# Attention output of a FoX layer: from three matmul passes over V to two, with an add behind

## The chip, the core and the metric

The kernel runs on one NeuronCore of a Trainium2 chip. Its time is the device time of one execution, in microseconds (us), and lower is better. The core's engines run side by side and meet only at semaphores: TensorE (PE in the rows; PEld is its weight load), VectorE (DVE), ScalarE (ACT), GpSimd (POOL) and the DMA queue of SyncE (SP).

## What is computed

Two layers on x of 1 x 512 x 1024 floats. Layer 0 mixes tokens by a Conformer convolution, layer 1 by the forgetting attention below; a squared-ReLU MLP of width 4096 follows each. There are 16 heads of 64 columns.

```python
def forgetting_attention(h, w_in, b_f, w_o):
    proj = h @ w_in
    q, k, v = proj[..., :D], proj[..., D:2*D], proj[..., 2*D:3*D]
    F = cumsum(log_sigmoid(proj[..., 3*D:] + b_f), axis=1)
    ...
    s = einsum("bhqd,bhkd->bhqk", q_blk, k) * HEAD_DIM ** -0.5
    s = s + (f_blk[..., None] - F[:, :, None, :])
    s = where(kpos <= qpos, s, -1e30)
    p = softmax(s, axis=-1)
    return einsum("bhqk,bhkd->bhqd", p, v)
    ...
    return o @ w_o
```

## The kernel before

Matmul operands are single precision, split in two: the high part (`...hi`) is a copy rounded to TensorE's reduced float format, and the rest (`...lo`) is the value minus that copy. ScalarE makes the high part, VectorE the rest, and a product is three passes on TensorE: high x high, high x rest, rest x high.

The attention takes heads in pairs. Pair 0 is written out (`PE_FIRST`, `ACT_FIRST`, `DVE_FIRST`), pairs 1 to 5 are a loop on each engine (`PE_PAIR` and so on), pairs 6 and 7 are written out again. These lists are the order in which an engine issues the steps of a pair; an engine never passes a step that waits. In a pair the scores are numbered i = 0 to 7: head i // 4, block of 128 queries i % 4. The steps are

- S i: TensorE makes the scores (L1137, L1138). VectorE adds the causal mask, moves them to `prob` and takes the maximum (L2452); ScalarE takes the exponential (L1737). TensorE may make S i only when VectorE has moved S i-2, since two banks of PSUM take turns.
- N i: VectorE normalises: a reciprocal, then a product that waits for it (L2440, L2443).
- T i: TensorE transposes the probabilities (L1170), ScalarE makes `pThi` (L1765), VectorE `pTlo` (L2484).
- V: TensorE transposes V of both heads into PSUM bank `OUTP`; VSPLIT makes `vhi` (ScalarE, L1742) and `vlo` (VectorE, L2460).
- O i: TensorE multiplies the probabilities of head i with V (L1180 to L1182), 128 output rows, of which the head uses its own 64. ScalarE copies them to `ohi` (L1771), VectorE writes the rest to `olo` (L2494). `o_ready` counts this; it frees bank `OUTP`.
- P, EVAC, SPLIT, PARTS, AGAIN: projection of q, k, v of the next pair, its evacuation (L2372 is EVAC 0), the split of weights (L1792 on VectorE), the parts of q and k (L1694, L1697, L1701, L1704 on ScalarE; L2377, L2390 on VectorE).

On VectorE the loop's list ends with O 0, T 6, T 7, SPLIT 1, PARTS 0, PARTS 1, O 1, and starts with EVAC 0, S 0, SPLIT 2, N 0, S 1, S 2, N 1, S 3. On ScalarE it ends with S 5, PARTS 0, S 6, S 7, AGAIN 0, T 4, T 5, PARTS 1, T 6, O 0, T 7, AGAIN 1, O 1. On TensorE it ends with T 4, O 0, T 5, P 8, T 6, P 9, T 7, P 10, P 11, O 1 and starts with P 0, S 0, S 1, P 1, S 2, P 2, T 0, S 3. ScalarE's T 4 of a pair waits until TensorE's O 0 is done, since it overwrites `pThi`.

Of the kernel before, what the change touches and what calls it, by code (L numbers as in the profile page):

```python
# [4 lines left out]
F32 = mybir.dt.float32  # L5
# [5 lines left out]
P = 128  # L11
# [146 lines left out]
def build(nc, x, g_mix_pre, g_mix_post, g_ffn_pre, g_ffn_post, conv_pw1_w, conv_pw1_b, conv_dw_w,  # L158
# [75 lines left out]
    def y_sums(j):  # L234
# [13 lines left out]
    vhi = put("vhi", [P, TB, P], F32R, aa)  # L248
    vlo = put("vlo", [P, TB, P], F32R, aa)
# [54 lines left out]
        "wf_hi wf_ready f_done f_z f_abs f_cum f_hi f_lo f_one f_part f_rows f_base f_ready sel sel_part "  # L304
        "pr_evac q_hi0 q_hi1 q_lo0 q_lo1 q_two0 q_two1 k_hi0 k_hi1 k_lo0 k_lo1 k_two0 k_two1 vtr v_hi v_ready "
        "sc_done sc_seen sc_evac ex_done rc_done p_ready t_done p_hi pt_ready pv_done o_hi o_ready stored"
# [59 lines left out]
    with nc.Block() as block:  # L366
# [3 lines left out]
        def _(sp):  # L370
# [101 lines left out]
        def _(pool):  # L472
# [145 lines left out]
            g.memset(fwork[:, FONE, :], 1.0).then_inc(s["f_one"], 1)  # L618
# [44 lines left out]
        def _(pe):  # L663
# [460 lines left out]
            def attention(p, project, order=PE_PAIR, fill={}):  # L1124
                for what, i in order:
# [47 lines left out]
                    if what == "O":  # L1173
# [3 lines left out]
                        for kb in range(TB):  # L1177
                            o = psum[:, OUTP, kb * P:S]
                            ph, pl = pThi[:, kb, kb * P:S], pTlo[:, kb, kb * P:S]
                            pe.matmul(o, vhi[:, kb, :], ph, start=kb == 0, stop=False)  # L1180
                            pe.matmul(o, vhi[:, kb, :], pl, start=False, stop=False)
                            mm = pe.matmul(o, vlo[:, kb, :], ph, start=False, stop=kb == TB - 1)  # L1182
# [34 lines left out]
        def _(act):  # L1217
# [513 lines left out]
            def attention(p, project, order=ACT_PAIR):  # L1731
                for what, i in order:
# [34 lines left out]
                    if what == "O":  # L1767
# [3 lines left out]
                        a.activation(dst, psum[rows, OUTP, :], ACT.Copy).then_inc(s["o_hi"], 1)  # L1771

# [12 lines left out]
        def _(dve):  # L1785
# [628 lines left out]
            dve.wait_ge(s["f_one"], 1)  # L2414
# [21 lines left out]
            def attention(p, project, order=DVE_PAIR):  # L2436
# [8 lines left out]
                for what, i in order:  # L2445
# [41 lines left out]
                    if what == "O":  # L2487
# [70 lines left out]
```

## Time and profile before

| | |
|---|---|
| median of 3 runs | 1161.71 us (1161.38 to 1161.81) |
| span of the profiled execution, first to last instruction | 1160.8 us |
| TensorE busy | 1140.7 us, 98% of the span |
| VectorE busy | 901.5 us, 78% |
| ScalarE busy | 668.2 us, 58% |
| attention, from pair 0's scores to its last O step | about 589 to 786 us of the span |

The page gives the profiled execution's span alone, and no separate time of its own: its span is 0.9 us below the median of the timed runs, which is what lies around the first and the last instruction. A busy share says how full an engine is over the whole span, not which engine is waited for in a stretch. A timeline row gives start, length, engine, line, operation, output and inputs with the shape, and in brackets the idle time before it with what ended it. Starts of neighbouring rows on one engine can be closer than the length of the first, since an instruction's end overlaps the next one's start.

### The profile page before, as it was taken

To read this page: it belongs to the slowest core of one execution; us is meant where nothing else is said; L and a number is where in the kernel's file an instruction comes from. 1 tells how busy PE (TensorE), PEld (TensorE's weight loads), DVE (VectorE), ACT (ScalarE), POOL (GpSimd) and SP (SyncE) were. 2 spreads that over 40 slices of the span, in tenths; PEclk is the share of its full clock that TensorE was granted. 3 is DMA by queue.
4 is the path that set the end of the run, shared out by engine and by line. 5 is a ranking of instruction groups with operands and counts; after the bars stand their busy time and mean duration, and the time that the engine had idled before them with its cause. 6 is when DMAs were issued, how large, how long until landed. Compare 5 with 4: busy or idle time off the path is not lost. (4 is left out here: it accounts for less than half of the span.)

```text
span 1160.8 us, 16330 instructions
## 1 busy us (share of the span) xinstructions
PE 1140.7 (98%) x5662; PEld 961.7 (83%) x5662; DVE 901.5 (78%) x1385; ACT 668.2 (58%) x1152; POOL 201.5 (17%) x190
## 2 busy tenths in 40 slices
PE   8999999999999999999999999999999999999997
PEld 7788888888888888888888888888888888888886
DVE  5899965788479588589788888884788488586698
ACT  6778867565444353445786667665565453443453
POOL 5688860300000000002420010100300000000003
PEclk9999989999999999999999999999999999999999
DMA  5322123321522414312122322222423414215301
GB/s 170 98 66 72 37 75 109 110 73 45 173 73 85 170 37 150 105 37 57 53 55 60 86 72 54 73 74 73 146 73 116 135 40 154 100 37 182 109 19 73
DMA packets 103676, 102.31 MB, mean 88 GB/s; under 512 B 4621, under 2 KB 86541, under 8 KB 103610
## 3 DMA queue, kind: packets, MB, share of 16 engines
q1 hardware_dynamic: 103532, 101.29, 27.4%
q8 instruction: 39, 0.64, 0.2%
q14 instruction: 27, 0.22, 0.1%
q10 hardware_dynamic: 78, 0.16, 0.0%
HBM read 99.34 MB, written 2.10 MB: 87 GB/s over the span
## 5 line engine op out<-in xcount | busy, mean ns | idle before, releaser
L672 PE MATMUL psum<-hhi,whi 128*128 128x512 f32 x760 | 300.2, 395 | 0.8 <-DVE wlo L1792 0.5
L674 PE MATMUL psum<-hhi,wlo 128*128 128x512 f32 x760 | 296.3, 390 | 0.0
L673 PE MATMUL psum<-hlo,whi 128*128 128x512 f32 x760 | 296.0, 390 | 0.0
L1247 ACT ACTIVATE whi<-mraw 128x1024 fp32r<-128x1024 f32 x176 | 185.4, 1055 | 142.9 <-PE psum L969 113.6
L1803 DVE TENSOR_TENSOR wlo<-mraw,whi 128x1024 fp32r<-128x1024 f32 x176 | 214.4, 1224 | 42.3 <-ACT whi L1247 42.3
L967 PE MATMUL psum<-whi,aop_hi 128*128 128x512 f32 x448 | 174.9, 390 | 0.0
L969 PE MATMUL psum<-whi,aop_lo 128*128 128x512 f32 x448 | 174.4, 389 | 0.0
L968 PE MATMUL psum<-wlo,aop_hi 128*128 128x512 f32 x448 | 174.3, 389 | 0.0
L674 PEld LDWEIGHTS psum<-hhi,wlo 128*128 128x128 f32 x760 | 142.6, 188 | 30.5
L672 PEld LDWEIGHTS psum<-hhi,whi 128*128 128x128 f32 x760 | 142.8, 188 | 29.4 <-issue 1.8
L673 PEld LDWEIGHTS psum<-hlo,whi 128*128 128x128 f32 x760 | 142.9, 188 | 28.0
L1514 ACT ACTIVATE pair<-tmp 128x512 f32<-128x512 f32 x64 | 40.4, 633 | 156.0 <-DVE tmp L2098 156.0
L2098 DVE SCALAR_TENSOR_TENSOR tmp<-psum,rinv 128x512 f32<-128x512 f32 x64 | 44.0, 690 | 78.5 <-PE psum L674 75.9
L969 PEld LDWEIGHTS psum<-whi,aop_lo 128*128 128x128 f32 x448 | 84.1, 188 | 17.5
L968 PEld LDWEIGHTS psum<-wlo,aop_hi 128*128 128x128 f32 x448 | 84.1, 188 | 17.3
L967 PEld LDWEIGHTS psum<-whi,aop_hi 128*128 128x128 f32 x448 | 84.1, 188 | 17.2
L1882 DVE SCALAR_TENSOR_TENSOR psum<-upad,vec,psum 128x512 f32<-128x512 f32 x116 | 78.1, 750 | 3.4 <-ACT psum L1378 3.4
L2152 DVE TENSOR_TENSOR mraw<-mraw 128x1024 f32<-128x1024 f32 x64 | 78.0, 1221 | 1.7
L679 PE MATMUL psum<-hhi,whi 128*128 128x256 f32 (+1 forms) x192 | 60.1, 313 | 3.5 <-DVE hlo L1809 2.9
L654 POOL TENSOR_TENSOR scal<-acc,gpost 128x512 f32<-128x512 f32 x6 | 7.6, 1288 | 306.8 <-DVE wlo L1803 304.4
L681 PE MATMUL psum<-hhi,wlo 128*128 128x256 f32 (+1 forms) x192 | 57.9, 301 | 0.0
L680 PE MATMUL psum<-hlo,whi 128*128 128x256 f32 (+1 forms) x192 | 57.8, 301 | 0.0
(266 smaller groups left out, 2003.3 us busy)
## 6 DMA issues: line engine op xcount, KB each, us to landing
mraw<-in_mlp_w_up SPq DMA_DIRECT2D x64, 512.0 KB, 5.1
mraw<-in_mlp_w_down SPq DMA_DIRECT2D x64, 512.0 KB, 4.5
wraw<-in_conv_pw_w SPq DMA_DIRECT2D x20, 512.0 KB, 4.5
wraw<-in_attn_w_in SPq DMA_DIRECT2D x16, 512.0 KB, 4.9
wraw<-in_attn_w_in SPq DMA_DIRECT2D x16, 256.0 KB, 3.1
wraw<-in_attn_w_o SPq DMA_DIRECT2D x8, 512.0 KB, 4.0
xin<-in_x SPq DMA_DIRECT2D x4, 512.0 KB, 6.8
wraw<-in_conv_pw_w SPq DMA_DIRECT2D x8, 256.0 KB, 6.7
```

The lines of the kernel that those rows point to most:

```text
L672: pe.matmul(o, whi[:, u, kb, :], xhi, start=start, stop=False)
L673: pe.matmul(o, whi[:, u, kb, :], xlo, start=False, stop=False)
L674: return pe.matmul(o, wlo[:, u, kb, :], xhi, start=False, stop=stop)
L679: pe.matmul(o, whi[:, u, kb, :], xh, start=start, stop=False, skip_group_check=True)
L681: return pe.matmul(o, wlo[:, u, kb, :], xh, start=False, stop=stop, skip_group_check=True)
L967: pe.matmul(o, ah, wh, start=kt == 0 and (not kept or c == 0), stop=False)
L968: pe.matmul(o, ah, wl, start=False, stop=False)
L969: return pe.matmul(o, al, wh, start=False, stop=kt == 3 and (not kept or c == CHUNKS - 1))
L1247: a.activation(split_unit(whi, e), raw_unit(c, e_), ACT.Copy).then_inc(s["m_hi"], 1)
L1803: d.tensor_tensor(split_unit(wlo, e), raw_unit(c, e_), split_unit(whi, e).bitcast(F32), ALU.subtract).then_inc(s["m_ready"], 1)
L1882: d.scalar_tensor_tensor(dst, upad[:, r, t:t + S], vcol(V_DW + t, j), src, ALU.mult, ALU.add).then_inc(s["tap"], 1)
L2152: d.tensor_tensor(to, to, mraw[:, p[PLUS[i]], half], ALU.add).then_inc(s["t_sum"], 1)
```

## The change

V's high parts and rests of one head stand side by side as one stationary tile (`vboth`, 64 + 64 columns): the head's own 64 output rows get high V, the other 64 rows get the rest of V. Two passes (with `pThi` and `pTlo`) then give both; before, three passes were made and the other head's rows thrown away. The other rows have to be added: ScalarE copies them to a new tile `cross`, and VectorE adds `cross` to `olo` in a second instruction, which waits for that copy and for its own first one. `o_ready` is counted only after the add. To find semaphores for this, `f_one` and `stored` are replaced by further counts of `sel_part` and `x_loaded0`, each used once, at the gates and at the output.

```diff
-    vhi = put("vhi", [P, TB, P], F32R, aa)
-    vlo = put("vlo", [P, TB, P], F32R, aa)
+    vboth = put("vboth", [P, 2, TB, 2, HD], F32R, aa)
+    cross = put("cross", [P, S], F32, aa)
...
+    def v_by_head(lo):
+        s_, h_ = HD, TB * P
+        off, step = (s_, h_ - s_) if lo else (0, h_ + s_)
+        return bass.AP(vboth, off, [[2 * h_, P], [step, 2], [P, TB], [1, HD]])
+    def v_tokens():
+        return psum[:, OUTP, :].rearrange("p (q h d) -> p h q d", h=2, d=HD)
...
-                            o = psum[:, OUTP, kb * P:S]
-                            ph, pl = pThi[:, kb, kb * P:S], pTlo[:, kb, kb * P:S]
-                            pe.matmul(o, vhi[:, kb, :], ph, start=kb == 0, stop=False)
-                            pe.matmul(o, vhi[:, kb, :], pl, start=False, stop=False)
-                            mm = pe.matmul(o, vlo[:, kb, :], ph, start=False, stop=kb == TB - 1)
+                            o, v = psum[:, OUTP, kb * P:S], flat(vboth[:, i, kb, :, :])
+                            pe.matmul(o, v, pThi[:, kb, kb * P:S], start=kb == 0, stop=False)
+                            mm = pe.matmul(o, v, pTlo[:, kb, kb * P:S], start=False, stop=kb == TB - 1)
...
                         a.activation(dst, psum[rows, OUTP, :], ACT.Copy).then_inc(s["o_hi"], 1)
+                        act.wait_ge(s["o_ready"], 2 * p + (i + 1))
+                        a.activation(cross[rows, :], psum[other[i], OUTP, :], ACT.Copy).then_inc(s["o_cross"], 1)
...
                         d.tensor_tensor(dst, psum[rows, OUTP, :], hi.bitcast(F32),
-                                        ALU.subtract).then_inc(s["o_ready"], 1)
+                                        ALU.subtract).then_inc(s["o_part"], 1)
+                        dve.wait_ge(s["o_cross"], 2 * p + (i + 1))
+                        dve.wait_ge(s["o_part"], 2 * p + (i + 1))
+                        d.tensor_tensor(dst, dst.bitcast(F32), cross[rows, :],
+                                        ALU.add).then_inc(s["o_ready"], 1)
```

VSPLIT's two instructions (L1742, L2460) keep their place and size and write through `v_by_head`. No step changes its place in a list. What each O step issues is longer on two engines. On VectorE, in the loop around step O 0 (N 7 ahead of it; T 6, T 7 and SPLIT 1 behind), before:

```order
L2443 TENSOR_SCALAR prob<-prob,rden 128x512 [waits rc_done]
L2488 ISA
L2494 ISA [waits o_hi]
L2494 TENSOR_TENSOR olo<-psum,ohi 64x512
L2484 TENSOR_TENSOR pTlo<-psum,pThi 128x3x128 [waits p_hi]
L2484 TENSOR_TENSOR pTlo<-psum,pThi 128x4x128 [waits p_hi]
L1791 REGISTER_ALU
L1792 TENSOR_TENSOR wlo<-wraw,whi 128x1024 [waits w_hi0]
```

and with the change, where lines are 8 to 14 further down:

```order
L2453 TENSOR_SCALAR prob<-prob,rden 128x512 [waits rc_done]
L2498 ISA
L2504 ISA [waits o_hi]
L2504 TENSOR_TENSOR olo<-psum,ohi 64x512
L2508 TENSOR_TENSOR olo<-olo,cross 64x512 [waits o_part,o_cross]
L2494 TENSOR_TENSOR pTlo<-psum,pThi 128x3x128 [waits p_hi]
L2494 TENSOR_TENSOR pTlo<-psum,pThi 128x4x128 [waits p_hi]
L1801 REGISTER_ALU
L1802 TENSOR_TENSOR wlo<-wraw,whi 128x1024 [waits w_hi0]
```

One more instruction stands between O 0's subtraction and T 6, with two waits. At the loop's end, around O 1 (the last of PARTS 1 ahead of it, EVAC 0 and S 0 of the next pair's code behind the branch), before:

```order
L2390 TENSOR_TENSOR kb<-tmp,ka 64x512 [waits k_hi1]
L2488 REGISTER_ALU
L2494 ISA [waits o_hi]
L2494 TENSOR_TENSOR olo<-psum,ohi 64x512
L2498 REGISTER_ALU
L2498 COMPARE_AND_BRANCH
L2372 SCALAR_TENSOR_TENSOR tmp<-psum,rinv 128x512 [waits q_lo1,q_two0,q_two1,q_lo0,unit0]
L2452 ISA prob,negmax<-psum,causal 128x128 [waits sc_done,t_done]
```

and now:

```order
L2400 TENSOR_TENSOR kb<-tmp,ka 64x512 [waits k_hi1]
L2498 REGISTER_ALU
L2504 ISA [waits o_hi]
L2504 TENSOR_TENSOR olo<-psum,ohi 64x512
L2508 TENSOR_TENSOR olo<-olo,cross 64x512 [waits o_part,o_cross]
L2512 REGISTER_ALU
L2512 COMPARE_AND_BRANCH
L2382 SCALAR_TENSOR_TENSOR tmp<-psum,rinv 128x512 [waits q_lo1,q_two0,q_two1,q_lo0,unit0]
L2462 ISA prob,negmax<-psum,causal 128x128 [waits sc_done,t_done]
```

The add stands ahead of the next pair's EVAC 0 and S 0. On ScalarE, around O 0 (T 6 ahead, T 7 and AGAIN 1 behind), before:

```order
L1765 ACTIVATE pThi<-psum 128x3x128 [waits t_done]
L1771 ISA [waits pv_done]
L1771 ACTIVATE ohi<-psum 64x512
L1761 REGISTER_ALU
L1765 ACTIVATE pThi<-psum 128x4x128 [waits t_done]
L1704 ACTIVATE ka<-tmp 64x512 x2
```

and now:

```order
L1773 ACTIVATE pThi<-psum 128x3x128 [waits t_done]
L1779 ISA [waits pv_done]
L1779 ACTIVATE ohi<-psum 64x512
L1781 ACTIVATE cross<-psum 64x512 [waits o_ready]
L1769 REGISTER_ALU
L1773 ACTIVATE pThi<-psum 128x4x128 [waits t_done]
L1712 ACTIVATE ka<-tmp 64x512 x2
```

The copy to `cross` stands between O 0's copy and T 7.

## Rows read from the trace of the kernel before

**Rows 1.** Part 1 of the page: busy us (share of the span) and instructions.

```profile
PE 1140.7 (98%) x5662; PEld 961.7 (83%) x5662; DVE 901.5 (78%) x1385; ACT 668.2 (58%) x1152; POOL 201.5 (17%) x190
```

**Rows 2.** Windows, one loop turn: us, busy (count) of PE, PEld, DVE, ACT, POOL; clock.

```profile
639.60:665.15 25.55, 25.55 (x138) 21.76 (x137) 21.19 (x54) 17.50 (x39) 2.08 (x2) 1.00 0.23 62
```

**Rows 3.** Timeline of TensorE, one O step and what follows: start us, length us.

```profile
661.95 0.39 PE L1180 MATMUL psum<-pThi,vhi 128*128 128x512 f32 x1
...
663.81 0.44 PE L672 MATMUL psum<-hhi,whi 128*128 128x512 f32 x1
```

**Rows 4.** Timeline of TensorE, step S 3 of pairs 1, 2, 6.

```profile
617.72 0.50 PE L1137 MATMUL psum<-ka,qa 128*128 128x512 f32 x1
...
643.27 0.48 PE L1137 MATMUL psum<-ka,qa 128*128 128x512 f32 x1
...
745.46 0.48 PE L1137 MATMUL psum<-ka,qa 128*128 128x512 f32 x1
```

**Rows 5.** Timeline of ScalarE, pair 2, steps T 4 to T 7.

```profile
655.60 0.62 ACT L1765 ACTIVATE pThi<-psum 128x128 fp32r<-128x128 f32 x2 [0.32 <-PE psum L1182]
...
657.95 0.58 ACT L1771 ACTIVATE ohi<-psum 64x512 f32 x1
659.38 0.60 ACT L1765 ACTIVATE pThi<-psum 128x512 fp32r<-128x512 f32 x1 [0.86 <-PE psum L1170]
```

**Rows 6.** Timeline of VectorE, pair 2, steps O 0 to O 1 and on.

```profile
642.53 0.42 DVE L2452 CUSTOM_DVE_ANT_0 prob<-psum,causal 128x256 f32<-128x256 f32 x1
...
658.68 0.68 DVE L2494 TENSOR_TENSOR olo<-psum,ohi 64x512 f32 x1 [1.41 <-ACT ohi L1771]
659.29 0.54 DVE L2484 TENSOR_TENSOR pTlo<-psum,pThi 128x384 fp32r<-128x384 f32 x1
660.02 0.69 DVE L2484 TENSOR_TENSOR pTlo<-psum,pThi 128x512 fp32r<-128x512 f32 x1 [0.19 <-ACT pThi L1765]
...
663.31 1.41 DVE L2390 TENSOR_TENSOR kb<-tmp,ka 64x512 fp32r<-64x512 f32 x2
664.85 0.69 DVE L2494 TENSOR_TENSOR olo<-psum,ohi 64x512 f32 x1
665.62 0.69 DVE L2372 SCALAR_TENSOR_TENSOR tmp<-psum,rinv 128x512 f32<-128x512 f32 x1
...
667.57 0.16 DVE L2440 RECIPROCAL rden<-den 128x1 f32<-128x1 f32 x1
667.76 0.29 DVE L2443 TENSOR_SCALAR prob<-prob,rden 128x128 f32<-128x128 f32 x1
```

**Rows 7.** Waits, 596 to 790 us: total us, times, longest.

```profile
ACT pThi L1765 <- PE psum L1182: 2.0, 6, 0.4
```

**Rows 8.** Timelines of ScalarE and VectorE, pair 0 and the start of pair 1.

```profile
606.45 0.58 ACT L1771 ACTIVATE ohi<-psum 64x512 fp32r<-64x512 f32 x1
606.93 0.99 ACT L1765 ACTIVATE pThi<-psum 128x256 fp32r<-128x256 f32 x2
...
607.32 0.42 DVE L2484 TENSOR_TENSOR pTlo<-psum,pThi 128x256 fp32r<-128x256 f32 x1 [0.41 <-ACT pThi L1765]
...
609.89 0.69 DVE L2484 TENSOR_TENSOR pTlo<-psum,pThi 128x512 fp32r<-128x512 f32 x1
...
617.23 0.42 DVE L2452 CUSTOM_DVE_ANT_0 prob<-psum,causal 128x256 f32<-128x256 f32 x1
```

**Rows 9.** Timelines of VectorE and TensorE, end of pair 6.

```profile
762.20 0.69 DVE L2484 TENSOR_TENSOR pTlo<-psum,pThi 128x512 fp32r<-128x512 f32 x1 [0.31 <-ACT pThi L1765]
...
764.36 1.40 DVE L2390 TENSOR_TENSOR kb<-tmp,ka 64x512 fp32r<-64x512 f32 x2
766.82 0.69 DVE L2494 TENSOR_TENSOR olo<-psum,ohi 64x512 fp32r<-64x512 f32 x1 [1.05 <-ACT ohi L1771]
767.54 0.29 DVE L2452 CUSTOM_DVE_ANT_0 prob<-psum,causal 128x128 f32<-128x128 f32 x1
...
767.90 0.44 PE L1137 MATMUL psum<-ka,qa 128*128 128x384 f32 x1 [0.54 <-DVE negmax L2452]
```

More of the change, by code:

```diff
@@ L303, in build @@
         "comb t22_done q_sum ss_done tot_done trms_done tinv_done tneg_done nrm_a nrm_d m1_tr m_tr x1_done h1_hi h1_ready x_tr gains cg tile_out "
-        "wf_hi wf_ready f_done f_z f_abs f_cum f_hi f_lo f_one f_part f_rows f_base f_ready sel sel_part "
+        "wf_hi wf_ready f_done f_z f_abs f_cum f_hi f_lo f_part f_rows f_base f_ready sel sel_part "
         "pr_evac q_hi0 q_hi1 q_lo0 q_lo1 q_two0 q_two1 k_hi0 k_hi1 k_lo0 k_lo1 k_two0 k_two1 vtr v_hi v_ready "
-        "sc_done sc_seen sc_evac ex_done rc_done p_ready t_done p_hi pt_ready pv_done o_hi o_ready stored"
+        "sc_done sc_seen sc_evac ex_done rc_done p_ready t_done p_hi pt_ready pv_done o_hi o_part o_cross o_ready"
     ).split()
@@ L466, in _ @@
                 sp.wait_ge(s["tile_out"], n)
-                sp.dma_start(od[t], flat(xtok[:, t, :, :])).then_inc(s["stored"], 16)
-            sp.wait_ge(s["stored"], 16 * TB)
+                sp.dma_start(od[t], flat(xtok[:, t, :, :])).then_inc(s["x_loaded0"], 16)
+            sp.wait_ge(s["x_loaded0"], 16 * (TB + 1))
         @block.gpsimd
@@ L617, in _ @@
             pool.wait_ge(s["m_unit"], MLP_UNITS)
-            g.memset(fwork[:, FONE, :], 1.0).then_inc(s["f_one"], 1)
+            g.memset(fwork[:, FONE, :], 1.0).then_inc(s["sel_part"], 1)
             g.memset(causal[:, :], 0.0).then_inc(s["f_base"], 1)
@@ L1741, in attention @@
                         act.wait_ge(s["pv_done"], 2 * p + 1)
-                        a.activation(flat(vhi[:, :, :]), psum[:, OUTP, :], ACT.Copy).then_inc(s["v_hi"], 1)
+                        a.activation(v_by_head(False), v_tokens(), ACT.Copy).then_inc(s["v_hi"], 1)
                     if what == "F":
@@ L2413, in _ @@
             dve.wait_ge(s["f_z"], 3)
-            dve.wait_ge(s["f_one"], 1)
+            dve.wait_ge(s["sel_part"], 10)
             d.tensor_tensor_scan(fwork[:, FCUM, :], fwork[:, FONE, :], fwork[:, FLOG, :], 0.0,
@@ L2459, in attention @@
                         dve.wait_ge(s["v_hi"], p + 1)
-                        d.tensor_tensor(flat(vlo[:, :, :]), psum[:, OUTP, :], flat(vhi[:, :, :]).bitcast(F32),
+                        d.tensor_tensor(v_by_head(True), v_tokens(), v_by_head(False).bitcast(F32),
                                         ALU.subtract).then_inc(s["v_ready"], 1)
```

## The prediction

> **What bounds the kernel now.** The page's first part comes first: TensorE is busy 98% of the span [rows 1]. A share over the whole span can't tell who is waited for in the attention, so I took the windows next. One turn of the loop over pairs lasts 25.55 us and TensorE is busy in all of it, at the full clock (1.00, the 2.4 GHz level) [rows 2]; S 3 of pairs 1, 2 and 6 stands 25.55 us apart per pair [rows 4]. Read so, a cut in TensorE's work is a cut in time. But VectorE is busy 21.19 us of the same 25.55, and the gaps between its instructions leave little of the rest free. So the third view is the timelines of VectorE and ScalarE over one turn, for what each idle time waits for, and how far TensorE stays behind its releases. There a second chain shows, nearly as long as TensorE's own work.
>
> The chain begins at TensorE's T 3 and runs in ScalarE's order (T 3, S 5, PARTS 0, S 6, S 7, AGAIN 0, T 4, T 5, PARTS 1, T 6, O 0), goes over to VectorE with the copy of O 0, runs in VectorE's order (O 0, T 6, T 7, SPLIT 1, PARTS 0, PARTS 1, O 1, EVAC 0, S 0, SPLIT 2, N 0, S 1), and ends at TensorE's S 3, which needs S 1 moved. From S 3 TensorE works down to T 3 again. It is slack in four places only. ScalarE's T 4 waits 0.32 us for TensorE's O 0 [rows 5], in all pairs about as much (2.0 us in 6 times) [rows 7]. VectorE's T 7 waits 0.19 for ScalarE. VectorE's O 1 starts at 664.85, where PARTS 1 ends at 664.72 and a next instruction could start 0.03 later: 0.10. And S 1 is moved at 642.53 + 0.42 = 642.95 [rows 6]; TensorE goes on 0.07 after such an end (767.54 + 0.29 to 767.90, where it did wait) [rows 9], so it could make S 3 at 643.02 and makes it at 643.27 [rows 4]: 0.25. Together 0.86 us a turn.
>
> **What the change takes away.** An O step lasts 661.95 to 663.81, 1.86 us for 12 matmuls [rows 3]. The third pass is one of three alike at each width, so 0.62 us goes from each, 1.24 a pair, 9.9 us over 16 heads. TensorE alone would need 25.55 - 1.24 = 24.31 us a turn. Nothing of the chain above runs through an O step, save ScalarE's wait of 0.32 at T 4: as O 0 ends 0.62 earlier, that wait goes.
>
> **What it adds.** ScalarE's copy to `cross` is of the kind and shape of the copy to `ohi`, 0.58 us [rows 5]. In the loop it is hidden: after O 0, ScalarE idles 0.86 before T 7 [rows 5], and after O 1 it is ahead of VectorE, whose S 0 it needs next. VectorE's add waits for it and does not wait long: the copy ends about 0.5 us after the first one's end, the subtraction takes 0.69.
>
> The add on VectorE is a 64 x 512 instruction like the subtraction (0.68) and like the two in `kb` (two in 1.41, so 0.72 from start to start) [rows 6]. It waits for VectorE's own result ahead of it. The nearest row for that is the reciprocal and its product: 0.16 long, the next starts 0.19 after its start [rows 6], 0.03 after its end, where T 6 starts 0.61 after O 0's start, ahead of its end. So the subtraction holds the add back 0.69 + 0.03 = 0.72, and what follows stands behind the add as it stood behind the subtraction: **0.72 us a head**. Bounds: 0.61, if the own wait costs nothing; 0.80, if two waits cost what the step to EVAC 0 with its five does (664.85 + 0.69 to 665.62: 0.08). I take 0.72, by the row that has this kind of wait.
>
> The Trainium skill (VectorE: DVE Perf Modes, section The DRAIN you can't avoid) says that a semaphore on each of a row of VectorE instructions cost nothing extra, measured on copies. By it the add would cost the 0.61 of the lower bound and the sum below would be 1.3 us less (1.1 in the loop, 0.2 in pair 0). The reciprocal's row speaks against it where the second reads what the first wrote.
>
> VSPLIT's two instructions keep 128 x 512 elements in another order; I take them at no cost, since `pTlo` is written in strided blocks too and takes 0.69 at 512 columns [rows 6]. On VectorE the wait for TensorE's S 7, which comes behind it, would take up a longer one; without that cover 0.1 us more would be 0.1 us a turn. The swapped semaphores are waited for once each; nothing.
>
> **The sum.** A turn: two adds, 1.44, less the 0.86 of slack, is 0.58 longer than now: 26.13 us. TensorE, with 24.31 of work, waits some 1.8 us a turn, at S 0, S 2 or S 3. The shorter O steps give nothing beyond the 0.32. From S 3 of pair 1 to S 3 of pair 6 are five turns: **+2.9** (0.61: +0.36 a turn, +1.8; 0.80: +0.74, +3.7).
>
> Pair 0, ahead of that, has another order, O 0 behind T 6 on VectorE and ahead of T 5 on ScalarE. There ScalarE's copy is not hidden: T 5 follows O 0 at once, 0.48 later [rows 8], so it moves 0.48, and VectorE's T 5 waits for it (0.41 idle). From that T 5 on, no row of VectorE lists an idle time down to S 1 of pair 1; T 7 moves by 0.48 + 0.72 = 1.20 and TensorE's O 1 behind it, and after the second add S 1 moves by **1.92**. TensorE's S 3 stands at 617.72 [rows 4], S 1's end 617.65 + 0.07 [rows 8]: no slack, so all counts. (1.70 with 0.61; 2.2 with 0.80 and 0.61 for ScalarE's step.)
>
> Pair 6 has more slack: besides T 4, T 7 waits 0.31 and O 1 waits 1.05 for TensorE [rows 9]. The first add is covered but for 0.72 - 0.33 - 0.31 = 0.08, PARTS 1 ends at 765.84, O 1's subtraction starts at 765.87 in place of 766.82, the second add takes back 0.72, and TensorE's S 2, now held by S 0, comes 0.23 earlier: **-0.2** (-0.5 if VectorE isn't late at all: -1.24 + 0.72; +0.1 if T 7's wait stays). In the last pair one add stands ahead of T 7, which O 1 needs, and one ahead of the last part of the output projection; against them two shorter O steps of 0.62: **0** (from -0.6 to +0.7).
>
> 1.92 + 2.9 - 0.2 + 0 = **+4.6 us**: the span goes from 1160.8 to 1165.4. The profiled execution has no other time on the page, and the median of the runs is 0.9 above its span; so 1166.3. With the lower ends (1.70 + 1.8 - 0.5 - 0.6) 1164.1, with the upper (2.2 + 3.7 + 0.1 + 0.7) 1168.4.
>
> **Rivals.**
> *TensorE stays the bound.* For it: its busy share, and its idle times, hardly any. Then all 9.9 us are won: 1151.8. For a gain that can be told from no change (below) the chain must have 1.44 + (2.3 + 1.7) / 5 = 2.2 us of slack a turn (1.7 for pairs 0 and 6), where I find 0.86; or the add would have to be far below any VectorE row of this size. Against it: the wait at S 2 in pair 7, where TensorE already waits 0.54 for VectorE's S 0 [rows 9]. The Trainium skill (Perfetto Trace Analysis, section Identifying the Most-Contended Engine) has the engine with the highest occupancy as the one to shorten. By that rule this rival's time follows. Chance 0.07.
> *The turn keeps its length.* The chain has 0.58 more slack than I found, by starts that I read as bound and aren't. Then pairs 0 and 6 alone count, +1.7: 1163.4. Chance 0.15.
> *The two readers of one bank hinder each other.* VectorE's subtraction and ScalarE's copy to `cross` read the two halves of bank `OUTP` at the same time, which no row of before shows. If one had to wait for the other, each add would start some 0.58 later, on the chain: 4.6 + 16 x 0.58 less what pairs 6 and 7 hide, about +12: 1174. Chance 0.06.
> The forecast: 0.72.
>
> **How the numbers follow.** A difference under 0.2% (2.3 us, 1159.4 to 1164.0) is about what this measurement can't tell from no change. The forecast's own range, 1164.1 to 1168.4, is slower; the second rival is within; the first is faster. Faster 0.07, same 0.16, slower 0.77. The range for 8 in 10 goes down into the second rival and up a little past the upper end: 1162.8 to 1168.8.
>
> **What would show it.** S 3 of neighbouring pairs some 26.1 us apart; in the list of waits TensorE's score matmuls waiting for VectorE's maximum, 1.5 to 2 us a pair; the add 0.69 long, 0.72 behind the subtraction; no wait of VectorE's T 7 left, and still one of over 1 us at O 0; ScalarE's T 4 not waiting for TensorE. It is wrong if TensorE's rows stay without gaps at S 0 to S 3, if VectorE's idle time in the loop is above 1.5 us a turn beside the wait at O 0, or if the subtraction or the copy of an O step is longer than 0.7 us.

## The result, and the profile after

The changed kernel takes 1167.93 us (median of 4 runs, 1166.18 to 1168.57) and the kernel before 1161.70 (median of 4, 1161.38 to 1161.81). The ratio is 1.005, with an interval of 1.0035 to 1.0064: slower by about 6 us, 0.5%, which is clear of the noise. The profiled run is the first of the four: 1168.03 us, its span 1166.3.

Some 1.5 us of the 6.2 come from a stretch far ahead of the attention, in which TensorE's clock stays low for longer in some runs of either kernel (last section): at an equal mean granted clock, 0.997, the changed kernel's one run takes 1166.18 us and the six of the kernel before beside the first four experiments have a median of 1161.5, which is **+4.7 us**, where +4.6 was forecast. One run is no measurement of its own; in the two traces the attention is 4.35 us longer (below).

The first part of the page, as in [rows 1]:

```profile
PE 1135.4 (97%) x5598; PEld 951.6 (82%) x5598; DVE 910.6 (78%) x1401; ACT 677.0 (58%) x1168; POOL 201.8 (17%) x190
```

TensorE has 64 matmuls less, VectorE and ScalarE 16 instructions more each. The window of one loop turn, from S 3 of pair 2 to S 3 of pair 3, as in [rows 2]:

```profile
646.75:672.85 26.10, 25.05 (x131) 20.48 (x129) 22.33 (x56) 18.60 (x41) 2.18 (x2) 1.00 0.23 60
```

The turn is 0.55 us longer, at the same full clock. VectorE has 1.1 us more to do in it, and TensorE is no longer busy throughout. TensorE's timeline shows where; L1147 makes scores, L1189 and L1190 are the O step, L682 the next projection (as in [rows 3, 4, 9]):

```profile
620.63 0.50 PE L1147 MATMUL psum<-ka,qa 128*128 128x512 f32 x1
...
646.75 0.50 PE L1147 MATMUL psum<-ka,qa 128*128 128x512 f32 x1
...
664.92 0.39 PE L1189 MATMUL psum<-pThi,vboth 128*128 128x512 f32 x1
...
666.13 0.44 PE L682 MATMUL psum<-hhi,whi 128*128 128x512 f32 x1
...
668.01 0.32 PE L1147 MATMUL psum<-ka,qa 128*128 128x128 f32 x1 [0.28 <-issue]
...
670.88 0.44 PE L1147 MATMUL psum<-ka,qa 128*128 128x384 f32 x1 [0.77 <-DVE negmax L2462]
...
672.85 0.50 PE L1147 MATMUL psum<-ka,qa 128*128 128x512 f32 x1
...
773.27 0.44 PE L1147 MATMUL psum<-ka,qa 128*128 128x384 f32 x1 [1.53 <-DVE negmax L2462]
```

S 3 rows stand 26.12 and 26.10 apart. O 1 is 1.21 us long (664.92 to 666.13), so 0.65 is saved. What was saved is lost at S 0 and S 2, which wait for VectorE, and in pair 7 S 2 waits 1.53 in place of 0.54. In the list of waits the cause has a row of its own:

```profile
PE psum L1147 <- DVE negmax L2462: 6.3, 7, 1.5
```

The brackets show only part of such a wait, since a matmul is drawn some 0.15 us beyond the point at which the next could start (0.39 long, with the next row 0.23 later, in O 1 of both kernels). The distances from the first row of a step to the first row of the next tell all of it. Worked out so from TensorE's timelines, for one loop turn, from S 3 of pair 2 to S 3 of pair 3 (the two kernels on the right are experiments, the first and the eleventh below), in us:

| step | before | after | no copies, no adds | one add, GpSimd's rows moved |
|---|---|---|---|---|
| T 1, up to S 5 | 0.16 | 0.16 | 0.61 | 0.16 |
| O 0 | 1.95 | 1.38 | 1.38 | 1.38 |
| O 1 | 1.86 | 1.21 | 1.21 | 1.21 |
| P 0, up to S 0 | 1.42 | 1.88 | 1.43 | 1.44 |
| P 1, up to S 2 | 1.37 | 2.32 | 1.37 | 1.38 |
| whole turn | 25.55 | 26.10 | 25.11 | 24.60 |

The O steps lose 0.57 and 0.65, some 1.2 us a turn, which would leave TensorE 24.34. The stalls ahead of S 0 and S 2 alone take 0.46 + 0.95 = 1.41.

VectorE after the change, pair 0 and pair 2 (line numbers differ from kernel to kernel; L2504 subtracts, L2508 is the add; as in [rows 6, 8]):

```profile
610.63 0.67 DVE L2504 TENSOR_TENSOR olo<-psum,ohi 64x512 fp32r<-64x512 f32 x1
611.41 0.68 DVE L2508 TENSOR_TENSOR olo<-olo,cross 64x512 fp32r<-64x512 f32 x1
...
661.80 0.68 DVE L2504 TENSOR_TENSOR olo<-psum,ohi 64x512 f32 x1 [1.41 <-ACT ohi L1779]
662.59 0.68 DVE L2508 TENSOR_TENSOR olo<-olo,cross 64x512 f32 x1
663.20 1.14 DVE L2494 TENSOR_TENSOR pTlo<-psum,pThi 128x384 fp32r<-128x384 f32 x2
664.26 1.21 DVE L1802 TENSOR_TENSOR wlo<-wraw,whi 128x1024 fp32r<-128x1024 f32 x1
...
668.37 0.69 DVE L2504 TENSOR_TENSOR olo<-psum,ohi 64x512 f32 x1
669.16 0.69 DVE L2508 TENSOR_TENSOR olo<-olo,cross 64x512 f32 x1
669.93 0.69 DVE L2382 SCALAR_TENSOR_TENSOR tmp<-psum,rinv 128x512 f32<-128x512 f32 x1
```

The add is 0.68 to 0.69 long and starts 0.79 behind the subtraction (0.78 to 0.81 in all 16). T 7 has no wait left; O 0 still waits 1.41 us for `ohi`. ScalarE, pair 0 and pair 2 (L1781 is the copy to `cross`; as in [rows 5, 7, 8]):

```profile
607.06 0.57 ACT L1779 ACTIVATE ohi<-psum 64x512 fp32r<-64x512 f32 x1
607.65 0.59 ACT L1781 ACTIVATE cross<-psum 64x512 f32<-64x512 f32 x1
608.27 0.77 ACT L1773 ACTIVATE pThi<-psum 128x256 fp32r<-128x256 f32 x2
...
658.79 0.55 ACT L1773 ACTIVATE pThi<-psum 128x128 fp32r<-128x128 f32 x2
...
661.07 0.58 ACT L1779 ACTIVATE ohi<-psum 64x512 f32 x1
661.67 0.59 ACT L1781 ACTIVATE cross<-psum 64x512 f32<-64x512 f32 x1
662.35 0.60 ACT L1773 ACTIVATE pThi<-psum 128x512 fp32r<-128x512 f32 x1
```

T 4 (658.79) waits no more. In the loop the copy lies where ScalarE idled ahead of T 7; in pair 0 it pushes T 5 to 1.21 us behind `ohi`, where it stood 0.48 behind. VSPLIT's two instructions, taken at no cost, kept their lengths (0.58 and 0.68).

### The profile page after: what moved, and what is told of

It is laid out like the page before. It is cut to its first block and busy times, and to the rows that moved or that the text cites. A ratio compares the mean times of both kernels' runs of the same rounds, so it can differ in the third digit from the quotient of the medians.

```text
span 1166.3 us, 16250 instructions
## 1 busy us (share of the span) xinstructions
PE 1135.4 (97%) x5598; PEld 951.6 (82%) x5598; DVE 910.6 (78%) x1401; ACT 677.0 (58%) x1168; POOL 201.8 (17%) x190
## 5 line engine op out<-in xcount | busy, mean ns | idle before, releaser
L682 PE MATMUL psum<-hhi,whi 128*128 128x512 f32 x760 | 300.2, 395 | 0.8 <-DVE wlo L1802 0.5
L682 PEld LDWEIGHTS psum<-hhi,whi 128*128 128x128 f32 x760 | 142.7, 188 | 29.7 <-issue 1.8
```

Of the source, the lines that this page charges most:

```text
L682: pe.matmul(o, whi[:, u, kb, :], xhi, start=start, stop=False)
```

## The experiments

The theory is that of the prediction: a chain over ScalarE and VectorE sets a turn, the adds stand in it, and TensorE's shorter steps only take up slack. The rivals are that TensorE is the bound and the adds merely hide its gain, and that the copies, the tiles or the semaphores cost what the adds are blamed for. In the table, "pair 0" is the distance of VectorE's S 0 from pair 0 to pair 1, "turn" that from pair 2 to pair 3, both from the start of the row; times are medians in us. The ratio and its 95% interval are those on record; the ratio is not the quotient of the two medians.

| kernel | time | before beside it | ratio | pair 0 | turn |
|---|---|---|---|---|---|
| before | | | | 25.75 | 25.52 |
| changed | 1167.93 | 1161.70 | 1.005 [1.0035, 1.0064] | 28.09 | 26.10 |
| 1 no copies, no adds | 1156.45 | 1162.19 | 0.9957 [0.9941, 0.9974] | 25.75 | 25.11 |
| 2 copies only | 1157.99 | 1162.19 | 0.9965 [0.9953, 0.9978] | 26.50 | 25.14 |
| 3 adds only | 1166.01 | 1162.19 | 1.0027 [1.0016, 1.0039] | 27.24 | 25.94 |
| 4 before, with adds | 1169.61 | 1162.19 | 1.0065 [1.0048, 1.0082] | 27.36 | 26.34 |
| 5 before, tiles moved | 1162.84 | 1161.94 | 1.0 [0.9991, 1.001] | 25.80 | 25.52 |
| 6 as 1, GpSimd's rows at S 7 | 1158.46 | 1161.94 | 0.9971 [0.9958, 0.9983] | 25.31 | 25.15 |
| 7 adds on GpSimd | 1163.18 | 1161.94 | 1.0006 [0.9996, 1.0016] | 27.26 | 25.47 |
| 8 as 7, copy and rows moved | 1169.57 | 1161.94 | 1.0061 [1.0044, 1.0078] | 26.15 | 26.67 |
| 9 as 1, GpSimd's rows at O 0 | 1154.79 | 1162.47 | 0.9938 [0.9921, 0.9954] | 25.83 | 24.60 |
| 10 one add in VectorE's idle time | 1159.45 | 1162.47 | 0.9977 [0.9968, 0.9987] | 26.53 | 25.13 |
| 11 as 10, GpSimd's rows at O 0 | 1157.62 | 1162.47 | 0.9955 [0.9938, 0.9971] | 26.07 | 24.61 |
| 12 as 11, copy of pair 0 moved | 1157.25 | 1161.29 | 0.9966 [0.9952, 0.9979] | 25.75 | 24.60 |

### 1 to 3: the copies and the adds apart

The first kernel leaves out both, the second the adds, the third the copies. In the second, ScalarE's copy no longer waits for `o_ready`, and TensorE waits for the copy before it writes the bank again; in the third, GpSimd zeroes `cross` once, and the first add of pair 0 waits for that.

```diff
 # 1 and 3: ScalarE, step O
-                        act.wait_ge(s["o_ready"], 2 * p + (i + 1))
-                        a.activation(cross[rows, :], psum[other[i], OUTP, :], ACT.Copy).then_inc(s["o_cross"], 1)
 # 1 and 2: VectorE, step O (o_ready is counted by the subtraction)
-                        d.tensor_tensor(dst, dst.bitcast(F32), cross[rows, :],
-                                        ALU.add).then_inc(s["o_ready"], 1)
 # 3: VectorE, step O
-                        dve.wait_ge(s["o_cross"], 2 * p + (i + 1))
```

> The changed kernel without ScalarE's copies to cross and without VectorE's adds; the products with the rest of V are made and left out of the output. Theory 1 (the chain of ScalarE and VectorE is the bound of a turn, and the adds alone made the kernel slower): the chain loses both adds and keeps the 0.86 us of slack that the shorter O steps give, so the S 3 of neighbouring pairs stand 24.7 us apart (25.55 before, 26.12 with the adds), five turns give -4.3 us, pairs 0, 6 and 7 about another -1: about 1156.4 us. Theory 2 (TensorE is the bound wherever VectorE does not hold it up by the adds): all 9.9 us come, turns of 24.31 us, 1151.8 us. Theory 3 (a turn keeps its length whatever TensorE saves): 25.55 us a turn and about 1161.5 us.

> The changed kernel with ScalarE's copies to cross and without VectorE's adds; the rest of V is left out of the output. Theory 1 (the adds carry the cost; in the loop a copy lies in ScalarE's wait ahead of T 7): turns of 24.7 us as without both, pair 0 about 0.5 us later through T 5, together about 1157 us. Rival (the copies hold up as much as the adds, as they stand in front of T 7 on ScalarE and in front of the end of a bank's use): turns of 25.3 us or more, and 1160 us or more.

> The changed kernel with VectorE's adds and without ScalarE's copies: the tile cross is zeroed once, the rest of V is left out of the output. Theory 1: turns of 26.12 us as in the changed kernel, pair 0 some 0.5 us earlier, about 1167 us. Rival (the copies share the cost): turns of 25.6 us or less and 1164 us or less.

Times and ranks came out as Theory 1 has them. For the first kernel's time that was partly luck: the five turns from S 3 of pair 1 gave 2.8 us and not 4.3 (127.74 to 124.95), and pairs 6 and 7 gave 2.2, up to the last O step, and not 1. Without adds the kernel is faster than before, with or without copies; with the adds alone it is slower, and the turn is 25.94, 0.16 short of the changed kernel's. The copies cost nothing in the loop (25.14 against 25.11) and 0.75 us in pair 0 (26.50 against 25.75).

Two things did not fit. First, the third kernel's add stands closer to the subtraction than in the changed kernel. VectorE's timeline there:

```profile
660.48 0.68 DVE L2505 TENSOR_TENSOR olo<-psum,ohi 64x512 f32 x1 [1.40 <-ACT ohi L1782]
661.20 0.69 DVE L2510 TENSOR_TENSOR olo<-olo,cross 64x512 f32 x1
```

That is 0.72, not 0.79. The add waits here for VectorE's own result alone; in the changed kernel it waits for the copy too, which has ended by then: in O 0 at 662.26, where the add starts at 662.59 above, in O 1 at 667.63, ahead of the subtraction itself. The second wait costs 0.07, twice a turn: nearly the whole of the 0.16. The third kernel shows it in itself as well: its first add of pair 0, the only one with a second wait, stands 0.78 behind (609.54 to 610.32).

Second, the first kernel's turn is 25.11, neither 24.7 nor 24.31. TensorE loses 0.45 us at T 1, up to S 5 (table above). T 1 waits for N 1, and VectorE's rows show why that is late; GpSimd's rows stand in the second fence:

```profile
666.69 1.04 DVE L2451 TENSOR_SCALAR prob<-prob,rden 128x256 f32<-128x256 f32 x1
...
674.54 0.69 DVE L2492 TENSOR_TENSOR pTlo<-psum,pThi 128x512 fp32r<-128x512 f32 x1
...
677.28 0.35 DVE L2451 TENSOR_SCALAR prob<-prob,rden 128x256 f32<-128x256 f32 x1
```

```profile
666.54 1.04 POOL L644 TENSOR_TENSOR qb<-gates_q,onehot 64x512 fp32r<-64x512 f32 x1 [16.73 <-PE psum L1148]
673.88 1.04 POOL L644 TENSOR_TENSOR qb<-gates_q,onehot 64x512 fp32r<-64x512 f32 x1 [6.30 <-PE psum L1148]
```

The product of N 1, 0.35 us long elsewhere, takes 1.04 when GpSimd has started 0.15 before it, and ends 0.15 after GpSimd. `pTlo` at 674.54 keeps its 0.69 beside GpSimd's second instruction: it has one input in PSUM. The Trainium skill (SBUF — State Buffer, section Who interferes with whom) says that VectorE and GpSimd share a pair of ports, that instructions of a fast two-port mode or with two inputs in SBUF contend for it, and that whoever comes second is blocked until the other's instruction ends. The rows agree, nearly to the length of the wait: the product loses 0.69 us, where 0.89 of GpSimd's instruction were left. That the product, with one tensor from SBUF, runs in such a mode is shown by no row. In the kernel before, and in the changed one, N 1 came ahead of GpSimd (643.92 against 644.18, and 673.66 against 673.77), and its product took 0.35. The first kernel itself has a turn without the collision, from pair 1 to pair 2: it is 24.59 long.

### 4: the kernel before, with the adds

```diff
 # VectorE, step O of the kernel before; cross is zeroed once
-                                        ALU.subtract).then_inc(s["o_ready"], 1)
+                                        ALU.subtract).then_inc(s["o_part"], 1)
+                        dve.wait_ge(s["o_part"], 2 * p + (i + 1))
+                        d.tensor_tensor(dst, dst.bitcast(F32), cross[rows, :],
+                                        ALU.add).then_inc(s["o_ready"], 1)
```

> The kernel before with its three passes, and only VectorE's add behind each subtraction put in, of a tile that was zeroed once: the result is that of the kernel before. Theory 1 (the shorter O steps of TensorE give back 0.32 us a turn, ScalarE's wait for O 0): two adds of 0.79 us less 0.54 us of slack make turns of 26.6 us, five turns +5.2, pair 0 +1.6, pair 6 some +0.5: about 1169 us. Rival (the two passes give nothing at all): the turn of the changed kernel, 26.12 us, and its time without the copies, about 1167 us or less. Second rival (the adds lie in idle time of VectorE, and something else in the change costs): 25.55 us a turn and 1162 us.

The turn is 26.34. Against the third kernel, which differs by the two passes and the layout of V alone, that is 0.40 more: with the adds in place TensorE's 1.2 us of savings are worth 0.40 a turn, against 0.32 forecast. The turn lies between the forecast (26.6) and its first rival (26.12), the time at the forecast: the adds alone make the kernel before 7.4 us slower.

### 5: what else the change does

```diff
+    cross = put("cross", [P, S], F32, aa)
-            g.memset(fwork[:, FONE, :], 1.0).then_inc(s["f_one"], 1)
+            g.memset(fwork[:, FONE, :], 1.0).then_inc(s["sel_part"], 1)
-            sp.wait_ge(s["stored"], 16 * TB)
+            sp.wait_ge(s["x_loaded0"], 16 * (TB + 1))
```

> The kernel before with only what the change does beside the attention: the tile cross is set aside (the tiles behind it move by its 2 KB), f_one and stored are replaced by further counts, o_part and o_cross exist and are not used. It computes all that the kernel before computes. Theory 1 (what the changed kernel loses lies in the attention; the 0.57 us ahead of it and the 0.46 us behind it in the profiled runs are differences between runs): the time of the kernel before to within 0.2%, 1161 to 1163 us. Rival (the moved tiles or the shared counts cost about 1 us outside of the attention): 1163 us or more.

The moved tiles and shared counts cost nothing that can be measured: the ratio is 1.0, and its interval leaves room for some 1 us either way. The median is 0.9 above the one beside it, so the time alone does not rule out the rival of about 1 us; the trace adds that pair 0 and the turn kept their lengths (25.80 and 25.52). One turn of it, from S 3 of pair 4 to S 3 of pair 5, is 26.05 us long. GpSimd has started 0.03 ahead of N 1's product there, so the collision of the first kernel can come up without the shorter O steps as well:

```profile
695.50 1.17 DVE L2444 TENSOR_SCALAR prob<-prob,rden 128x256 f32<-128x256 f32 x1
```

### 6 and 9: GpSimd's rows at another time

GpSimd writes rows of `qb` for the next pair, those of head 0 when S 3 is done (where N 1 is due), those of head 1 when S 7 is done. In the sixth kernel both wait for S 7, in the ninth those of head 0 come last and wait for ScalarE's `ohi` of O 0.

```diff
 # 6
-                    pool.wait_ge(s["sc_done"], 8 * p + (4 * hh - 4))
+                    pool.wait_ge(s["sc_done"], 8 * p)
 # 9, in the place of the loop over hh
+                pool.wait_ge(s["sc_done"], 8 * p)
+                head_rows(2 * p + 1, 1)
+                pool.wait_ge(s["o_hi"], 2 * p - 1)
+                head_rows(2 * p, 0)
```

> The kernel without copies and adds (the rest of V is left out of the output), and GpSimd's rows for head 0 of the next pair wait for S 7 of the pair and not for S 3. Without adds a turn was 25.11 us and not 24.7, with TensorE waiting at S 5 and S 2 for some 0.7 us; VectorE's product of N 1 took 1.04 us there and 0.35 us in the kernel before, beside GpSimd's rows, which start 0.15 us ahead of it. Theory A (GpSimd holds up that product, and nothing else is left in a turn): TensorE without waits, 24.4 us a turn (25.54 less the 1.16 that the O steps lose), five turns -3.5 us: about 1153 us. Theory B (with that gone the chain of ScalarE and VectorE ends the turn, as predicted): 24.7 us, about 1154.5 us. Rival (the stretched product is no cause): 25.1 us and 1156.4 us.

The sixth kernel missed: 1158.46, and a turn of 25.15, which is the rival's. But its cause is not the rival's: the product of N 1 takes 0.35 in every turn, and T 1, up to S 5, is back at 0.16 in four turns of five (0.27 in the other). The collision had moved. VectorE's SPLIT 0 and GpSimd's two instructions:

```profile
675.76 1.98 DVE L1800 TENSOR_TENSOR wlo<-wraw,whi 128x1024 fp32r<-128x1024 f32 x1
```

```profile
674.51 2.15 POOL L644 TENSOR_TENSOR qb<-gates_q,onehot 64x512 fp32r<-64x512 f32 x2 [23.13 <-PE psum L1148]
```

SPLIT 0 has both inputs in SBUF and takes 1.22 us elsewhere; GpSimd is done at 676.66. N 5, behind SPLIT 0 on VectorE, comes later, and so does TensorE's T 5: from the first row of O 0 to that of T 5 it takes 1.91 us in place of 1.38.

> The kernel without copies and adds (the rest of V is left out of the output), with GpSimd's rows for head 0 of the next pair behind those for head 1, waiting for ScalarE's ohi of O 0. The rows at S 7 held up VectorE's SPLIT 0 in the place of N 1 (1.44 us in the mean for a split in that run), and the turn stayed at 25.16 us. VectorE is in operations that read PSUM (the subtraction of O 0, T 6, T 7) for 1.8 us behind ohi, and such operations kept their length beside GpSimd in every run. Theory A (the collisions of GpSimd with VectorE's operations from SBUF to SBUF are what is left): TensorE without waits, 24.4 us a turn, some -3.5 us against 1156.5, about 1153 us. Theory B (with that gone the chain of ScalarE and VectorE ends the turn): 24.7 us, about 1154.5 us. Rival (another wait of 0.6 us in a turn takes the place once more): 25.1 us, 1156.5 us.

Here the turn is 24.60, between A and B, and the time 1154.79. Of the 1.2 that the O steps lose, 0.92 arrives. Two small waits of 0.1, at S 2 and S 3, are most of what is still held back, and S 2 and S 3 wait for VectorE's S 0 and S 1. So the bound that was left in the first kernel was the collision. Behind it the chain ends the turn again, by then only some 0.25 us above TensorE's own 24.34.

### 7 and 8: the adds on GpSimd

```diff
 # GpSimd, behind its rows of pair p; the adds of pair p - 1
+                    pool.wait_ge(s["o_cross"], 2 * p + (i + 1 - 2 * back))
+                    pool.wait_ge(s["o_part"], 2 * p + (i + 1 - 2 * back))
+                    g.tensor_tensor(dst, dst.bitcast(F32), cross[rows, :], ALU.add).then_inc(s["o_ready"], 1)
 # TensorE, ahead of V, in the place of o_ready
+                            pe.wait_ge(s["o_part"], 2 * p)
+                            pe.wait_ge(s["o_cross"], 2 * p)
```

> The changed kernel with the add moved from VectorE to GpSimd, behind its rows for the heads; TensorE's next use of the bank waits for the subtraction and the copy, and only the products with W_o wait for the add. All is computed. Theory 1 (the adds cost only by their place on VectorE): a turn of 25.13 us as with the copies alone, and 0.4 to 0.6 us more at the end, where the last add is waited for: about 1158.5 us. Rival (GpSimd's adds stretch VectorE's operations beside them, as its rows stretch the product of N 1): turns of 25.5 us or more, and 1160.5 us or more.

> As the one before, and ScalarE's copy to cross of O 0 comes behind its T 7, and GpSimd's rows for head 0 wait for S 7. All is computed. Theory A (nothing is left on TensorE's way in a turn): turns of 24.4 to 24.5 us, pair 0 not later than without copies, and some 0.5 us more at the last add: about 1153.5 us. Theory B (the chain of ScalarE and VectorE ends a turn): 24.7 us, about 1155 us. Rival (GpSimd and VectorE hold each other up elsewhere): 25.1 us or more, 1157.5 us or more.

Both missed, and the rivals hold: 1163.18 and 1169.57, turns of 25.47 and 26.67. In the seventh the adds meet SPLIT 1 and SPLIT 2 of VectorE:

```profile
687.44 1.53 DVE L1821 TENSOR_TENSOR wlo<-wraw,whi 128x1024 fp32r<-128x1024 f32 x1
...
693.41 1.78 DVE L1821 TENSOR_TENSOR wlo<-wraw,whi 128x1024 fp32r<-128x1024 f32 x1
```

```profile
686.59 1.29 POOL L656 TENSOR_TENSOR olo<-olo,cross 64x512 f32 x1 [7.20 <-DVE olo L2523]
692.82 1.29 POOL L656 TENSOR_TENSOR olo<-olo,cross 64x512 f32 x1 [4.93 <-DVE olo L2523]
```

0.31 and 0.56 us are lost on VectorE, in the chain, and they make up the turn: 24.60, as in the ninth kernel without any collision, + 0.87 = 25.47. In the eighth the later copy brings the add behind the start of SPLIT 1, and then GpSimd is the one that waits (2.19 us where it took 1.29), holds up the parts of q for 0.98 us more (2.38 for two that take 1.40), and meets SPLIT 2 as well; GpSimd's rows at S 7 meet SPLIT 0, as in the sixth (1.99).

```profile
689.74 1.22 DVE L1823 TENSOR_TENSOR wlo<-wraw,whi 128x1024 fp32r<-128x1024 f32 x1
690.99 2.38 DVE L2408 TENSOR_TENSOR qa<-tmp,qa 64x512 fp32r<-64x512 f32 x2
```

```profile
689.92 2.19 POOL L656 TENSOR_TENSOR olo<-olo,cross 64x512 f32 x1 [7.65 <-ACT cross L1802]
```

### 10 to 12: one add, where VectorE waits

One add of 128 rows serves both heads, and it stands in front of O 0 of the next pair, where VectorE waits 1.4 us for `ohi`. Pairs 6 and 7 add at their own end. The eleventh kernel has GpSimd's rows as in the ninth, the twelfth moves ScalarE's copy in pair 0 behind T 7.

```diff
-            ("T", 4), ("T", 5), ("N", 7), ("O", 0), ...
+            ("T", 4), ("T", 5), ("N", 7), ("X", 1), ("O", 0), ...
 # VectorE
+                    if what == "X":
+                        q = p - i
+                        ...
+                        d.tensor_tensor(dst, dst.bitcast(F32), cross[:, :], ALU.add).then_inc(s["o_ready"], 1)
 # 12, ScalarE's list of pair 0
-             ("T", 7), ("AGAIN", 1), ("O", 1)]
+             ("T", 7), ("X", 0), ("AGAIN", 1), ("O", 1)]
```

> The changed kernel with one add of 128 rows for both heads in the place of two of 64, and put in front of O 0 of the next pair, where VectorE waits 1.4 us for ohi; pairs 6 and 7 add at their own end, since the products with W_o wait for it. TensorE's next use of the bank waits for subtraction and copy alone. All is computed. Theory 1 (an add costs only where it stands in the chain, and the wait for ohi covers it): turns of 25.13 us as with the copies alone; against the copies alone (1158.0 us) an add at the end of pair 6 and one at the end of pair 7, 0.8 us each: about 1159.5 us. Rival (the wait is no cover, since O 0 is late by the add or the add meets GpSimd): turns of 25.7 us or more, 1162.5 us or more.

> As the one before, and GpSimd's rows for head 0 behind ohi of O 0. All is computed. Theory A: turns of 24.4 us, about 1156 us. Theory B: 24.7 us, about 1157.5 us. Rival (another wait takes the place): 25.1 us, 1159.5 us.

> As the one before, and in pair 0 ScalarE's copy to cross of O 0 comes behind its T 7 and not in front of T 5. All is computed. Theory (in pair 0 the copy of O 0 stands in front of T 5 and T 6, which VectorE and TensorE wait for): S 0 of pair 1 comes 25.4 to 25.8 us behind that of pair 0, and not 26.1 to 26.5; 0.5 us less than before, about 1157 us. Rival (the copy costs as much behind T 7, where it holds up the second copies of k for pair 1): no change, 26.1 to 26.5 us and 1157.6 us.

1159.45, 1157.62 and 1157.25 us: all three faster than the kernel before, by 0.2 to 0.5%. The tenth and the twelfth came out as their first theory has it. The eleventh missed Theory A (24.4 and 1156): its turn of 24.61 lies between A and B and its time at B's 1157.5. VectorE and GpSimd in the eleventh kernel:

```profile
681.08 0.68 DVE L2510 TENSOR_TENSOR olo<-olo,cross 128x512 f32 x1
682.57 0.68 DVE L2518 TENSOR_TENSOR olo<-psum,ohi 64x512 f32 x1 [0.81 <-ACT ohi L1786]
683.17 1.28 DVE L2502 TENSOR_TENSOR pTlo<-psum,pThi 128x384 fp32r<-128x384 f32 x2
684.37 1.22 DVE L1810 TENSOR_TENSOR wlo<-wraw,whi 128x1024 fp32r<-128x1024 f32 x1
```

```profile
682.59 1.04 POOL L645 TENSOR_TENSOR qb<-gates_q,onehot 64x512 fp32r<-64x512 f32 x1 [6.27 <-ACT ohi L1786]
```

The add takes 0.6 of the 1.4 us that O 0 waited, and 0.81 are left: it is free. GpSimd is done at 683.63, while VectorE is at rests that it takes from PSUM, ahead of SPLIT 1. The turn is 24.61, as without any copy and add. In the twelfth, pair 0 is at 25.75, the value of the kernel before: the copy of pair 0 had cost 0.32 in the eleventh and 0.78 in the tenth. The time falls by less than the runs can tell apart; against the kernel before beside each, the ratio of the twelfth is not lower than that of the eleventh.

## Why the prediction was right

**The mechanism.** The chain, and not TensorE, sets a turn. S 3 is 26.10 to 26.12 apart where 26.13 was forecast, and the stalls stand where they were placed, at S 0 and S 2. Shown by the second and the fourth kernel: taking the adds out alone makes the changed kernel faster than the one before, and the adds alone make the kernel before slower.

**The adds.** 0.79 a head, not 0.72: 1.58 a turn in place of 1.44. The term for the wait on VectorE's own result was right, 0.72 in the third kernel; the second wait, for a copy that has ended by then, came on top with 0.07, just inside the upper bound of 0.80. From start to start it is 0.61 from the add to T 6, which does not wait for VectorE's own result, 0.72 with that wait, and 0.79 with that wait and a second. The Trainium skill's statement, measured on copies, that a semaphore costs nothing extra (VectorE: DVE Perf Modes, section The DRAIN you can't avoid) does not hold for this pair.

**The slack.** 1.03 a turn, not 0.86: 26.10 is 25.55 + 1.58 - 1.03. By its places: from S 3 to ScalarE's `ohi` of O 0 14.68 us before [rows 4, 5] and 14.32 after (646.75 to 661.07), 0.36 where the wait at T 4 was put at 0.32; from T 6 to SPLIT 1 1.33 before (T 6 at 659.29 [rows 6], SPLIT 1 at 660.62) and 1.06 after (663.20 to 664.26), 0.27 where T 7 was put at 0.19; O 1 0.10 and S 3 0.25 as forecast; 0.05 is spread over other starts. SPLIT 1 of before:

```profile
660.62 1.22 DVE L1792 TENSOR_TENSOR wlo<-wraw,whi 128x1024 fp32r<-128x1024 f32 x1
```

These 0.17 and the 0.14 of the adds are of opposite sign: that the turn was right to 0.03 is partly luck.

**Pair 0.** S 3 of pair 1 comes 2.91 later (617.72 to 620.63), and 0.57 of that was there at S 0 of pair 0 (589.66 to 590.23 on VectorE, the rows below): 2.34, where 1.92 was forecast. The copy's step was mis-sized: T 5 moves by 0.73 (0.48 to 1.21 behind `ohi`), not 0.48, since the copy ends before T 5 starts while `ohi` and T 5 overlapped. 0.75 for the copies (second kernel) and two adds of 0.79 make 2.33.

```profile
589.66 0.29 DVE L2452 CUSTOM_DVE_ANT_0 prob<-psum,causal 128x128 f32<-128x128 f32 x1 [0.25 <-PE psum L1138]
```

```profile
590.23 0.29 DVE L2462 CUSTOM_DVE_ANT_0 prob<-psum,causal 128x128 f32<-128x128 f32 x1 [0.26 <-PE psum L1148]
```

**The loop, pairs 6 and 7.** S 3 of pair 6 is 5.56 later (745.46 to 751.02): less the 2.91 the five turns gave +2.65, forecast +2.9; the last of them is 25.97 long. S 2 of pair 7 is 5.37 later (767.90 to 773.27): -0.2, as forecast. TensorE's last part of the output projection, which waits for the last add, starts 4.92 later (787.45 to 792.37), so -0.45 in the last pair, forecast 0 with -0.6 as the lower end. The attention as a whole: 4.92 - 0.57 = +4.35, forecast +4.6. That these are so near is again partly luck: pair 0 came out 0.42 above its term, the five turns 0.25 and the last pair 0.45 below. The last part's first row, before and after (and S 3 of pair 6 after, ahead of it):

```profile
787.45 0.39 PE L672 MATMUL psum<-ohi,whi 128*128 128x512 f32 x1
```

```profile
751.02 0.49 PE L1147 MATMUL psum<-ka,qa 128*128 128x512 f32 x1
...
792.37 0.50 PE L682 MATMUL psum<-ohi,whi 128*128 128x512 f32 x1
```

**The rest of the 6.2 us** was not in the sum. The spans of the two profiled executions differ by 5.5: 4.35 in the attention, 0.57 ahead of it, where the first loads came later, and 0.58 behind. Of the 0.58, 0.11 is TensorE's start after its wait for the last add, and 0.47 lies at the very end, where the four stores of the output land 3.2 us after their issue (median) in place of 2.7. This goes with the kernels: it is 2.7 in all eight traces without an add on VectorE, and 3.3 in the other five with one. In those six traces, and in no other, a transfer of the queue q14, which loads instructions, falls among the last stores, 4 to 7 us before the end. That this transfer is the cause was not tried. The fifth kernel, where a store takes 2.7, shows that the moved tiles and counts are not. And the 0.9 us put between span and time were mis-read, since they set the span of one execution against the time of others: in every run that lists both, they are 1.7 to 2.1 apart, so the profiled execution of before took about 1 us longer than the median.

**The rivals.** TensorE as the bound is refuted in the changed kernel and, in an unexpected way, without the adds too: 0.41 of 1.2 us came, until GpSimd was moved out of the way; then 0.92. Beside the adds, TensorE's shorter steps alone were worth 0.40 a turn (third and fourth kernel). The engine with the highest share, 98% busy and 83% by its weight loads, was the one that the Trainium skill (Perfetto Trace Analysis, section Identifying the Most-Contended Engine) would have had shortened. That the turn keeps its length is refuted (+0.55). That two readers of one bank hinder each other is refuted: VectorE's subtraction takes 0.67 to 0.69 beside the copy. Of the signs named, two were mis-sized. TensorE's waits in the list are 1.05 us a turn (26.10 - 25.05), since rows are drawn longer than the step from one start to the next; by starts they are 1.8 (26.10 - 24.34). And one sign of being wrong did show: VectorE is idle for 26.10 - 22.33 = 3.77 us a turn, 2.36 beside the 1.41 at O 0, where over 1.5 was named. By the same count it was 2.95 before. Some 1.9 of the 2.36 lie between S 3 and O 0, where the chain runs over ScalarE; the longest, 0.60, waits for TensorE's S 7. The sign asked too much of VectorE's whole turn, and the mechanism doesn't rest on it.

## What to carry to other kernels

Before work is taken from an engine that looks full, look for the chain beside it and add up its slack; work that is put on that chain in exchange costs all of its length, less the slack. If it must be added, put it where its engine already waits for something later than its own inputs, and do it once for several parts: the adds cost 7.4 us behind each subtraction (fourth kernel); done once a pair in front of the next O 0, they cost nothing in the loop (25.13 against 25.14 a turn with the copies alone), and some 1.5 us in the whole kernel (1159.45 against 1157.99), with the adds of pairs 6 and 7 at their own ends. A shift of a few tenths can also bring VectorE and GpSimd into each other's way, so look at both after every gain that is smaller than it should be.

## What was not expected of the hardware

- VectorE and GpSimd hold each other up nearly to the end of the other's instruction, in both orders: N 1's product went from 0.35 to 1.04 us, SPLIT 0 from 1.22 to 1.98, and GpSimd's add from 1.29 to 2.19 where VectorE came first. VectorE's instructions with an input in PSUM were as long beside GpSimd as elsewhere, in every trace (`pTlo` at 512 columns at most 0.69).
- A wait for a semaphore that was already set cost VectorE 0.06 to 0.07 us when it stood beside the wait for its own last result (0.78 to 0.79 against 0.72).
- TensorE's clock falls in one stretch of every trace, and not equally long. The window 160 to 165 us of before, changed and first kernel (us, busy of the engines, granted clock, share of DMA, GB/s):

```profile
160.00:165.00 5.00, 5.00 (x28) 5.00 (x28) 4.47 (x12) 3.65 (x9) 3.77 (x7) 0.58 0.68 214
```

```profile
160.00:165.00 5.00, 5.00 (x25) 5.00 (x26) 4.22 (x12) 3.94 (x8) 4.35 (x8) 0.52 0.66 213
```

```profile
160.00:165.00 5.00, 5.00 (x39) 5.00 (x38) 4.85 (x12) 3.84 (x8) 3.36 (x6) 0.86 0.62 200
```

  The code is the same there. Part of each window is granted the 1.2 GHz level (0.50 in the windows of 1 us from 159 to 161 us of all three), after TensorE made 32 matmuls of a single column from 154 us on. Together with 0.57 us that the first loads came later in the changed kernel's profiled run, this makes VectorE's S 0 of pair 0 start anywhere from 587.9 to 590.2 us in these runs, as much as half the effect studied; distances within the attention are free of it. What decides how long the clock stays low was not tried.
